# Weight-block sums of a seven-product MLP, moved from VectorE to adding DMAs

## The reference, cut to what matters

```python
def _squared_relu_mlp(h, w1, w2):
    return jnp.square(jax.nn.relu(h @ w1)) @ w2      # w1 (1024, 4096), w2 (4096, 1024)

for layer in range(DEPTH):                           # DEPTH = 2
    h = _rms_norm(x, norm_mix_g[layer])
    x = x + mixer(h)
    h = _rms_norm(x, norm_ffn_g[layer])
    x = x + _squared_relu_mlp(h, ffn_w_in[layer], ffn_w_out[layer])
return _rms_norm(x, final_g)
```

## Time and profile before

| | us |
|---|---|
| median of 3 runs | 1365.18 (1363.27 to 1365.7) |
| the profiled execution | 1364.82 |
| its span, first to last instruction | 1363.0 |
| PE busy | 1345.2 |
| DVE busy | 802.0 |
| ACT busy | 577.3 |
| POOL busy | 54.9 |

### The profile page before, as it was taken

The page is one execution under the profiler, slowest core; times in us unless marked ns, Lnnn a source line. Parts: engine busy times, 40 slices in busy tenths (PEclk is TensorE's granted clock), DMA queues, the critical chain, the costliest instruction groups (busy, mean ns, idle before and its releaser), DMA issues. The chain is left out here.

```text
span 1363.0 us, 16831 instructions
## 1 busy us (share of the span) xinstructions
PE 1345.2 (99%) x6590; PEld 1123.0 (82%) x6590; DVE 802.0 (59%) x985; ACT 577.3 (42%) x842; POOL 54.9 (4%) x75
## 2 busy tenths in 40 slices
PE   8999999999999999999999999999999999999997
PEld 6788888898887887879888888888889888788786
DVE  6466455567758576685344344434366766848667
ACT  5556444344445344443333313323335444444443
POOL 3121000000000000000000000000000000000000
PEclk9999999999999999999999999999999999999999
DMA  8222221620513306123222232232232060411502
GB/s 262 83 63 61 88 78 39 216 94 31 185 63 109 108 31 216 32 82 122 91 78 78 71 102 79 72 108 77 92 124 94 31 216 32 154 63 52 195 0 78
DMA packets 92146, 131.14 MB, mean 96 GB/s; under 512 B 6696, under 2 KB 56104, under 8 KB 91952
## 3 DMA queue, kind: packets, MB, share of 16 engines
q1 hardware_dynamic: 90544, 124.44, 27.6%
q0 software_dynamic: 1536, 5.78, 1.4%
HBM read 128.09 MB, written 2.11 MB: 96 GB/s over the span
## 5 line engine op out<-in xcount | busy, mean ns | idle before, releaser
L624 PE MATMUL bank<-w,a_ring 128*128 128x512 f32 x1344 | 311.6, 391 | 2.9 <-DVE x L1525 2.5
L624 PEld LDWEIGHTS bank<-w,a_ring 128*128 128x128 f32 x1344 | 251.9, 188 | 60.6 <-DVE x L1525 8.8
L608 PE MATMUL bank<-hT_hi,w 128*128 128x512 f32 x896 | 277.1, 389 | 0.0
L608 PEld LDWEIGHTS bank<-hT_hi,w 128*128 128x128 f32 x896 | 168.2, 188 | 34.9
L1331 DVE TENSOR_TENSOR w<-raw,w 128x1024 fp32r<-128x1024 f32 x112 | 135.1, 1221 | 86.8 <-ACT w L1035 86.8
L608 PE MATMUL bank<-hT_lo,w 128*128 128x512 f32 x448 | 174.3, 389 | 0.0
L1287 DVE TENSOR_TENSOR w<-raw,w 128x1024 fp32r<-128x1024 f32 x96 | 120.7, 1259 | 87.1 <-ACT w L980 86.8
L527 PE MATMUL bank<-w,hT_hi 128*128 128x512 f32 x512 | 158.2, 390 | 0.0
L1043 ACT ACTIVATE hf<-bank 128x512 f32<-128x512 f32 x64 | 38.3, 598 | 209.9 <-PE bank L608 197.8
L1035 ACT ACTIVATE w<-raw 128x1024 fp32r<-128x1024 f32 x112 | 115.4, 1051 | 15.1 <-DVE raw L1481 9.3
L980 ACT ACTIVATE w<-raw 128x1024 fp32r<-128x1024 f32 x96 | 99.8, 1054 | 31.4 <-PE bank L527 28.4
(11 more groups left out here) (139 smaller groups left out, 1781.1 us busy)
## 6 DMA issues: line engine op xcount, KB each, us to landing
raw<-in_odd_w_in SPq DMA_DIRECT2D x96, 256.0 KB, 2.9
raw<-in_ffn_w_in SPq DMA_DIRECT2D x32, 512.0 KB, 3.9
arena<-in_ffn_w_in SPq DMA_DIRECT2D x32, 512.0 KB, 7.9
raw<-in_ffn_w_out SPq DMA_DIRECT2D x32, 512.0 KB, 5.0
arena<-in_ffn_w_out SPq DMA_DIRECT2D x32, 512.0 KB, 4.5
raw<-in_even_w_in SPq DMA_DIRECT2D x48, 256.0 KB, 3.4
raw<-in_odd_w_out SPq DMA_DIRECT2D x32, 256.0 KB, 2.7
x<-in_x SPq DMA_DIRECT2D x8, 512.0 KB, 6.5
```

The lines of the kernel that those rows point to most:

```text
L608: mm = pe.matmul(bank[w1_bank(g, j)][:, :], stat, hT[b][:, k, :], start=(k == 0 and i == 0), stop=(k == KT - 1 and i == 2))
L624: mm = pe.matmul(bank[first + t][:, :], a_ring[:, a_slot(g, i), a, k, P * t:P * t + P], w_slots[use_slot(g, 4 + i)][:, b, k, :], start=(st ...
```

## The change

The four sums of weight blocks in each chunk leave DVE. POOL issues for each a DMA from SBUF to SBUF of 128 rows of 8 KB that adds what it moves to its destination (`accum_op=ALU.add`). Since such a DMA can only add, the signs are moved: the scheme runs on A with its second block column negated and on B with B12 and B21 negated, so that T1 = B11 + B12, T2 = T1 + B22, T3 = B12 + B22 and T4 = B21 + T2 up to signs; S1 becomes A21 - A22, S4 becomes A12 + S2 up to sign, and the products with a True in the new last column of the table are subtracted from the residual. T3 is now made second, once T1 has landed, since it overwrites B12. Each sum has a semaphore of its own, which a landing raises by 16; ACT's copies and SP's loads wait for those, SP also for the low half of T2. The sums of layer 0 stand in POOL's program after the powers of the second norm, those of layer 1 after the powers of the fourth.

```diff
-PRODUCTS = ((2, True, (-1, 6), (-1, 1), (0, 0)),
+PRODUCTS = ((2, True, (-1, 6), (-1, 1), (0, 0), False),
...
-            (2, False, (0, 0), (-1, 4), (0, 1)),
+            (2, False, (0, 0), (-1, 4), (0, 1), True),
...
-        t_made = sem("t_made")
+        t_made = {i: sem(f"t_made{i}") for i in (T1, T2, T4, T3)}
...
-                                sp.wait_ge(t_made, 4 * (g - 1) + 3)
+                                sp.wait_ge(t_made[T4], 16 * g)
+                                sp.wait_ge(m_lo, 2 * use_of(g - 1, 4 + T2) + 2)
...
-                made = {4 + T1: 1, 4 + T2: 2, 4 + T4: 3, 4 + T3: 4}.get(i)
-                if made:
-                    act.wait_ge(t_made, 4 * g + made)
+                if i - 4 in (T1, T2, T4, T3):
+                    act.wait_ge(t_made[i - 4], 16 * g + 16)
...
-                    nc.vector.tensor_tensor(s_tmp, a21, a22, ALU.add).then_inc(s_made, 1)
+                    nc.vector.tensor_tensor(s_tmp, a21, a22, ALU.subtract).then_inc(s_made, 1)
...
-                nc.vector.tensor_tensor(v, bank[PRODUCTS[i][0] + t][:, :], v, ALU.add).then_inc(p_added, 1)
+                product = bank[PRODUCTS[i][0] + t][:, :]
+                if PRODUCTS[i][5]:
+                    nc.vector.tensor_tensor(v, v, product, ALU.subtract).then_inc(p_added, 1)
+                else:
+                    nc.vector.tensor_tensor(v, product, v, ALU.add).then_inc(p_added, 1)
...
                 w_lo_both(g, 4 + B21)
-                weight_sum(g, T1)
                 w_lo_both(g, 4 + T1)
-                weight_sum(g, T2)
                 w_lo_both(g, 4 + T2)
-                weight_sum(g, T4)
-                weight_sum(g, T3)
...
+            def weight_sums(g):
+
+                landed(g, 2)
+                pool.wait_ge(m_lo, 2 * use_of(g, 4 + B11) + 2)
+                pool.dma_start(raws[0], raws[2], accum_op=ALU.add).then_inc(t_made[T1], 16)
+                landed(g, 3)
+                pool.wait_ge(t_made[T1], 16 * g + 16)
+                pool.dma_start(raws[2], raws[3], accum_op=ALU.add).then_inc(t_made[T3], 16)
+                pool.wait_ge(m_lo, 2 * use_of(g, 4 + T1) + 2)
+                pool.dma_start(raws[0], raws[3], accum_op=ALU.add).then_inc(t_made[T2], 16)
+                pool.wait_ge(t_made[T2], 16 * g + 16)
+                pool.dma_start(raws[1], raws[0], accum_op=ALU.add).then_inc(t_made[T4], 16)
+
+            for g in range(CHUNKS):
+                weight_sums(g)
             load_gain(2)
...
             inv_std(3)
+            for g in range(CHUNKS, 2 * CHUNKS):
+                weight_sums(g)
             load_gain(4)
```

More of the change, by code:

```diff
@@ L401, in quarter @@
                     if c < 2:
-                        sp.wait_ge(t_made, 4 * (CHUNKS - 1) + 3)
+                        sp.wait_ge(t_made[T4], 16 * CHUNKS)
+                        sp.wait_ge(m_lo, 2 * use_of(CHUNKS - 1, 4 + T2) + 2)
                     else:
@@ L612, in product @@
             def product(g, i, t):
-                first, starts, (dg, before), _, _ = PRODUCTS[i]
+                first, starts, (dg, before), _, _, _ = PRODUCTS[i]
                 if g % CHUNKS or dg == 0:
@@ L1468, in _ @@
             hT_parts(1, TT - 1)
[L1471 to L1491, removed]
             def operand_sum(g, which):
@@ L1506, in operand_sum @@
                     dve.wait_ge(a_lo, 7 * g + S2 + 1)
-                    nc.vector.tensor_tensor(a12, a12, s_tmp, ALU.subtract).then_inc(s_made, 1)
+                    nc.vector.tensor_tensor(a12, a12, s_tmp, ALU.add).then_inc(s_made, 1)
                 else:
@@ L1773, in _, with landed @@
             inv_std(1)
+            def landed(g, i):
+                for half in range(2):
+                    pool.wait_ge(m_landed[2 * i + half], 16 * (2 * g + 2))
+            def weight_sums(g):
[11 more added lines that the diff above has]
+                weight_sums(g)
             load_gain(2)
```

## The result

The changed kernel takes 1373.4 us (median of 4 runs, 1372.59 to 1374.91) against 1365.35 before: ratio 1.0063, 95% interval [1.0046, 1.0081]. It is slower by 8.0 us, a third of the 23 that were forecast, and the second rival (1371) was nearer than the forecast (1388).

A forecast was written before the change was run, and what follows sets the result against it. PE, 99% busy, was taken as the bound, so relieving DVE gives 0; late T2 stalls PE 1.6 us in six chunks and 6.7 in two, together 23, so 1365.2 + 23 = 1388 us, range 1364 to 1465 (0.8).

The forecast's parts named there:

- the second rival: Adding transfers read twice at the best rate, b = 5.5; only the first chunks stall, 5.6 us: 1371 us, chance 0.10.
- The bound: PE is busy 99% of the span and has no waits for weight sums, so taking them off DVE is worth 0.
- The price of one transfer: Each 1 MB adding DMA: 1.1 us until data flow, b of flow taken as 6.8, 0.5 to landing.
- b: Data flow time of one 1 MB adding transfer: taken as 6.8 us, ends 3.4 and 10.2.
- When T2 must be there: Before each chunk's first product: T2 may land until 6.15 us before it, in chunk 1 at 401.4.
- When T2 is there: In chunk 1 T2 lands at 403.0 after T1 and T3, 1.6 us late, and PE stands for 1.6 us.
- 3b + 3.2: Time from the end of B11's low half on DVE to T2's landing, in us, T2 queued behind T3.
- the prediction's own sum: Six chunks x 1.6 = 9.6 us, two x 6.7 = 13.4; together 23. The two first chunks stall 3b - 13.7 each.
- The chunks: Six chunks stall 3b - 18.8, 1.6 us each; chunks 0 and 4, with less room, 3b - 13.7, 6.7 us each.

The follow-up runs named there:

- the swap alone: The kernel before, with the first half of product 3 added to the residual ahead of S3's low part on DVE: 1360.51 us, ratio 0.9965.
- the halves: The changed kernel with each sum in two transfers of 512 KB with their own semaphores, T2 ahead of T3: 1365.95 us, ratio 1.0005.
- T2 first: The changed kernel with POOL issuing T2's transfer ahead of T3's: 1369.42 us, ratio 1.0038.
- T3 twice: The changed kernel with T3's adding transfer issued twice, the second after the first landed, T2 behind both: 1432.1 us, ratio 1.0494.
- the filled gap: The changed kernel with 15 matmuls on zeros in PE's gap of chunk 0 only, before its wait for A11: 1372.1 us, ratio 1.0055.

## Why the prediction was partly right

By its own steps:

The bound. Right: PE at 99%, nothing to win on DVE. The kernels with less on DVE show it.

The price of one transfer. This is the step that failed. b was put at 6.8, twice the 3.4 us that POOL's load of the decay table took from first packet to last; in the same terms it measured 5.4 (7.0 us to landing, less 1.6). The mechanism, about two passes, agrees with the runs; the term was mis-sized because those 3.4 us hold idle time of the DMA engines (share 0.86), of which an addition has none (0.99). With 5.4 in place of 6.8 the prediction's own sum is 2 x (16.2 - 13.7) = 5 us in place of 23. The second rival, 5.5 us from the best rate of a stretch, had the right price and gave 1371. That it comes so near to 1373.4 is in part luck: it lacks POOL's 1.1 us a first chunk and the clock (both below), and about half of these is given back.

When T2 must be there. Right to 0.2 us: 5.93 to 5.97 measured against 6.15.

When T2 is there. The form 3b + 3.2 was right, with the order T1, T3, T2 in the queue, as the swap of T2 and T3 shows. With b = 5.4 it gives 19.4; measured from B11's low half at 302.05 to 323.01 are 20.96. POOL is 1.1 of the difference: 0.6 us from the semaphore to T1's issue and 0.5 from T1's landing to T3's, which the prediction left out. The other 0.4 us stays open.

The chunks. Six chunks were to stall 1.6 us each: none has a gap above 0.1, and 9.6 us of the forecast fell away. Chunk 1 has 1.8 us of room, chunks 2 and 5 have none. Two were to stall 6.7 and stalled 3.7. That they are the ones with less room was right, and is where the whole loss sits.

What was missed. The clock: the gap of chunk 0 costs 1.43 us more, and the 0.50 of a spell behind it stands behind the gap of chunk 4 too. Against that 0.7 us a first chunk come back. In this profile, then, the delay against the kernel before is 4.6 us at the end of chunk 0, and layer 1 adds 4.7 in chunk 4. Between the layers 1.45 us are won: the profile of before has its clock at 0.88 and 0.78 in two stretches after the pause at the norm, and this one has 1.00. The profiles of the swap alone and of the halves have 0.80 and 0.66 in a stretch there, so it comes and goes; I don't count it as an effect of the change.

## What to carry to other kernels

A sum moved from a busy engine to DMAs changes 2.3 us of work into 7 us of latency; look for the first place that has to wait for the chain of them, count the transfers that stand in its queue ahead, and read the room in the tightest iteration, not in the typical one. Price a transfer from the time that it keeps the DMA engines busy, not from its first packet to its last, and take a row with the same two memories at its ends where there is one. Where the bounding engine has no wait for the relieved one, look at its few waits by name instead: one swap of two instructions was worth more here than 73 us taken off DVE.

## What was not expected of the hardware

T1's transfer takes 2.2 us longer in chunks 2 and 5 than in chunk 1, in the changed kernel and in those with T2 first and with T3 twice. With the filled gap it is chunk 3 instead, by the same 2.2 us, and not 2 or 5; so it is not bound to a place in the program. POOL's rows of T1 and T3 in chunks 2 and 3 of the changed kernel:

```profile
467.17 0.87 POOL L1764 DMA_DIRECT2D raw<-arena  x1 [61.90 <-DVE w L1333]
476.89 0.87 POOL L1767 DMA_DIRECT2D arena<-arena  x1 [8.86 <-DMA raw<-arena]
...
549.76 0.87 POOL L1764 DMA_DIRECT2D raw<-arena  x1 [59.64 <-DVE w L1333]
557.62 0.87 POOL L1767 DMA_DIRECT2D arena<-arena  x1 [6.99 <-DMA raw<-arena]
```

T3's issue follows T1's by 9.7 us in chunk 2 and by 7.9 in chunk 3, and chunk 2's first product starts 0.25 us later against the kernel before than chunk 1's. In chunk 2 the data have all moved in time. What is late is the last of 16 tiny packets at the transfer's end; its semaphore counts 16. The DMA queues of the changed kernel from 473.5 to 474, from 474 to 475 and from 475 to 475.5 us (packets, MB, share):

```profile
q0 software_dynamic: 15, 0.00, 4.5%
q8 instruction: 1, 0.02, 5.9%
q0 software_dynamic: 1, 0.00, 0.3%
```

Fifteen come before 474, then a packet of 16 KB of instructions passes, and the sixteenth comes behind it; POOL goes on at 476.89. A packet of q8 lies in the same place, 7.1 to 7.2 us after the issue, in all seven transfers of T1 that are 2.2 us late in these four kernels. That the last packet waits behind it fits the rows; nothing was run to show it.
